# A long fp32 transformer kernel: the order of its steps planned by strands and kept durations in place of hand-set rates

## The reference

```python
# first_block: one layer
h = rmsnorm(x, norm1_g); proj = h @ w_in          # q, k, v (8 heads of 64), f_logit, u
attn = forgetting_attention(q, k, v, cumsum(log_sigmoid(f_logit + b_forget)))   # causal
pool = multiscale_pool(u, w_pool, pool_scale)     # trailing means over 2, 4, 8, 16 tokens
x = x + concat([attn, pool]) @ w_out
h2 = rmsnorm(x, norm2_g); x = x + (silu(h2 @ w_gate) * (h2 @ w_up)) @ w_down     # 2816 hidden
x = rmsnorm(x, final_g)
# second_block: layer 0 with diff_attention (8 heads, two maps each), layer 1 with mla_attention (16 heads, latents)
for i in (0, 1):
    x = x + (diff_attention, mla_attention)[i](rms_norm(x, attn_norm_g[i]))
    x = x + conv_ffn(rms_norm(x, ffn_norm_g[i]))  # up, causal convolution of 3 taps, silu(g) * val, down; 2816 hidden
return rms_norm(x, final_norm_g)
```

## Time and profile before

| what | value |
|---|---|
| median of 3 runs | 1991.57 us (1990.54 to 1992.43) |
| profiled execution, own time | 1996.32 us |
| its span, first to last instruction | 1994.2 us |
| mean granted TensorE clock | 0.971 of full speed |
| PE busy | 1884.0 us, 8953 matmuls |
| DVE, ACT, POOL busy | 1126.4, 793.9, 159.3 us |
| DMA | 152 MB, 76 GB/s over the span |

### The profile page before, as it was taken

How to read it: one execution, slowest core, us unless ns; L and a number is a source line. 1 busy time by engine, 2 the same in 40 slices (tenths; PEclk the granted TensorE clock), 3 DMA queues, 4 the chain that set the end, 5 groups by cost and what they waited for, 6 DMA issues and landing times.

```text
span 1994.2 us, 23116 instructions
## 1 busy us (share of the span) xinstructions
PE 1884.0 (94%) x8953; PEld 1551.3 (78%) x8953; DVE 1126.4 (56%) x1886; ACT 793.9 (40%) x1406; POOL 159.3 (8%) x155
## 2 busy tenths in 40 slices
PE   7997999999999899988999999998888799999998
PEld 6786778888887788877888888787777678888886
DVE  4557644344345666686663654646676676557365
ACT  4444432122234454443442432446545354234142
POOL 3002110000004100102000000023000020000001
PEclk9999999999999999988999999998898999999998
DMA  4211222332322112111322223221011022223322
GB/s 140 71 59 43 64 85 95 95 95 95 94 92 83 59 49 73 53 32 44 106 92 92 92 95 95 86 75 48 23 43 32 23 93 93 92 92 94 95 95 74
DMA packets 127769, 152.17 MB, mean 76 GB/s; under 512 B 9322, under 2 KB 98956, under 8 KB 127660
## 3 DMA queue, kind: packets, MB, share of 16 engines
q1 hardware_dynamic: 127384, 150.59, 23.9%
q10 hardware_dynamic: 276, 0.10, 0.0%
HBM read 148.50 MB, written 2.10 MB: 76 GB/s over the span
## 4 chain that ended last, share of the span: by engine, by line
PE 82%; DVE 8%; ACT 5%; issue 3%; POOL 2%; DMA 0%; SPq 0%; POOLq 0%; DVEq 0%; ACTq 0%
PE bk L1360 21%; PE bk L1361 21%; PE bk L1362 21%; PE bk L1388 4%; PE bk L1389 4%; PE bk L1390 4%; PE bk L1365 3%; DVE SM L1552 1%; ACT FS L1729 1%; DVE PT L1499 1%; POOL FS L1784 1%; ACT R L1668 1%; ACT WH L1664 1%; DVE R L1499 1%; DVE XT L1505 1%
## 5 line engine op out<-in xcount | busy, mean ns | idle before, releaser
L1360 PE MATMUL bk<-R,WH 128*128 128x512 f32 x1812 | 726.0, 401 | 16.4 <-DVE R L1499 10.9
L1361 PE MATMUL bk<-R,WH 128*128 128x512 f32 x1812 | 719.7, 397 | 0.0
L1362 PE MATMUL bk<-R,WL 128*128 128x512 f32 x1812 | 719.6, 397 | 0.0
L1494 DVE TENSOR_TENSOR WL<-RAW,WH 128x1024 fp32r<-128x1024 f32 (+3 forms) x282 | 352.7, 1252 | 634.5 <-ACT WH L1664 632.5
L1664 ACT ACTIVATE WH<-RAW 128x1024 fp32r<-128x1024 f32 (+3 forms) x282 | 293.8, 1042 | 641.4 <-PE bk L1362 589.1
L1360 PEld LDWEIGHTS bk<-R,WH 128*128 128x128 f32 x1812 | 342.7, 189 | 101.4 <-issue 20.2
L1362 PEld LDWEIGHTS bk<-R,WL 128*128 128x128 f32 x1812 | 342.2, 189 | 83.9
L1361 PEld LDWEIGHTS bk<-R,WH 128*128 128x128 f32 x1812 | 342.7, 189 | 80.3
L1388 PE MATMUL bk<-WH,R 128*128 128x512 f32 (+4 forms) x528 | 191.4, 362 | 7.8 <-DVE R L1486 4.3
L1784 POOL TENSOR_TENSOR FS<-FS 128x512 f32<-128x512 f32 x56 | 89.2, 1595 | 1341.4 <-ACT FS L1688 1338.3
L1389 PE MATMUL bk<-WH,R 128*128 128x512 f32 (+4 forms) x528 | 183.2, 347 | 0.0
(11 more groups left out here) (126 smaller groups left out, 1702.9 us busy)
## 6 DMA issues: line engine op xcount, KB each, us to landing
RAW<-in_ffn_w_up_dram SPq DMA_DIRECT2D x176, 256.0 KB, 3.0
RAW<-in_ffn_w_down_dram SPq DMA_DIRECT2D x44, 512.0 KB, 3.7
RAW<-in_w_gate_dram SPq DMA_DIRECT2D x44, 256.0 KB, 2.9
RAW<-in_w_up_dram SPq DMA_DIRECT2D x44, 256.0 KB, 3.1
RAW<-in_w_down_dram SPq DMA_DIRECT2D x22, 512.0 KB, 3.7
RAW<-in_da_w_qkv_dram SPq DMA_DIRECT2D x32, 256.0 KB, 3.0
RAW<-in_w_in_dram SPq DMA_DIRECT2D x17, 256.0 KB, 3.2
RAW<-in_w_out_dram SPq DMA_DIRECT2D x8, 512.0 KB, 3.6
```

Source lines behind the costliest of these rows:

```text
L1360: e.matmul(dst, lh, rh, start=start, stop=False)
L1361: e.matmul(dst, lh, rl, start=False, stop=False)
L1362: return e.matmul(dst, ll, rh, start=False, stop=stop)
L1494: e.tensor_tensor(WL[:, s, 0:m], RAW[:, r, 0:m], WH[:, s, 0:m].bitcast(F32), ALU.subtract).then_inc(on["wlo_dve"], 1)
```

## The change

The steps and what they compute stay. What appends them is replaced. Every line of work becomes a strand, a generator that yields its next step with all that the step waits for: one for each attention unit, for each map's max and exp, for each head's value product and output, for each evicted bank, for each turned head, for the high and the low weight halves, and one, `products`, that runs through all dense products from the first to the last. For every engine the plan keeps a time at which it is free (`free_at`), and for every semaphore value a time at which it is reached (`ready_at`), from durations kept for each kind of step (`takes`) and fixed delays (`LAG`, `HIDDEN`). `run` asks every strand for the beginning of its next step, takes the earliest, and among the steps of the same engine that could begin within `PATIENCE` of it the one of lowest rank: 0 for gates, norms and the reservation of tiles, 1 for attention, evictions and turns, 2 for weight halves and squares, 3 for `products`. Within a rank the strand that was made first wins. Steps that held several engines in turn (`root`, `gate_in`, `lam`) are cut into one step for each engine. Products may hold 5 of the 8 banks in attention stages (8 elsewhere) and other steps 4. An attention unit may begin when no more than `lag` units are between it and the last one turned. Tiles for queries, values and outputs are reserved in the order of the groups.

The diff, cut to its core; lines that only pass such strands on are left out:

```diff
...
-    "square": {"act": 1}, "acc": {"pool": 1}, "sums": {"pe": 1}, "root": {"dve": 5, "act": 2},
+    "square": {"act": 1}, "acc": {"pool": 1}, "sums": {"pe": 1}, "root_in": {"dve": 1}, "root_exp": {"act": 2}, "root_out": {"dve": 4},
...
+LAG = {"pe": 100.0, "act": 40.0, "dve": 40.0, "pool": 120.0}
+HIDDEN = {"pe": 0.0, "act": 85.0, "dve": 80.0, "pool": 0.0}
+PATIENCE = {"pe": 100.0, "act": 60.0, "dve": 60.0, "pool": 0.0}
...
+def takes(kind, eng, f):
+
+    def mm(n):
+        return max(110.0, n / 2.19)
+
+    def act(n, cols=0):
+        return 170.0 + 93.0 * cols + 0.83 * n
+
+    def dve(n):
+        return 150.0 + 1.04 * n
+    if eng == "pe":
+        if kind == "gemm_f":
+            return 3 * len(f["xs"]) * mm(512)
...
+        return {"wlo": 1273.0, "add": 682.0, "tap1": 743.0, "tap0": 743.0, "settle": 745.0, "diag": 880.0, "root_in": 165.0,
...
-        later, lates = [], []
-
-        def tick():
-            while lates:
-                lates.pop(0).both()
-
-        def pump(n=1):
-            tick()
-            for _ in range(n):
-                if later:
-                    later.pop(0)()
...
+        def begins(eng, after):
+            return max([free_at[eng]] + [at_time(d) + LAG[eng] for d in after])
+
+        def emit(kind, **fields):
+            t = None
+            for eng, n in SIGNALS[kind].items():
+                name = f"{kind}_{eng}"
+                fields[eng + "0"] = made.get(name, 0)
+                made[name] = fields[eng + "0"] + n
+                newest[eng] = fields[eng] = (on[name], made[name])
+                if n:
+                    t = max(t or 0.0, begins(eng, fields.get("after", ())))
+                    t += takes(kind, eng, fields)
+                    ready_at[id(on[name]), made[name]] = t
+                    free_at[eng] = t - HIDDEN[eng]
+            st = Step(kind, fields)
+            steps.append(st)
+            return st
...
+        def spawn(gen, rank=1):
+            serial[0] += 1
+            strands.append(Strand(gen, (rank, serial[0])))
...
+                can = []
+                for s in strands:
+                    if s.next is not None:
+                        eng = next(iter(SIGNALS[s.next[0]]))
+                        can.append((begins(eng, s.next[1].get("after", ())), eng, s))
+                if not can:
+                    assert not strands, [s.gen.__qualname__ for s in strands]
+                    break
+                t, eng, _ = min(can, key=lambda x: (x[0], x[2].rank))
+                s = min((x for x in can if x[1] == eng and x[0] <= t + PATIENCE[eng]), key=lambda x: x[2].rank)[2]
+                kind, fields = s.next
+                s.go(emit(kind, **fields))
+                if s.over:
+                    strands.remove(s)
+
+        tiles, fsl, banks = Ring(NT), Ring(NFS), Ring(NB)
+        taken = {"gemm": 0, "one": 0}
+        cap = {"gemm": NB, "one": 4, "kept": 0}
+
+        def bank(use="one"):
+            while not banks.fr or taken[use] >= cap[use]:
+                yield None
+            taken[use] += 1
+            b = banks.get()
+            b.use = use
+            return b
...
+            hi = yield step("hi", dst=dst_h, src=src, scale=1.0 if scale is None else scale, after=counts([*after, *free]))
+            lo = yield step("lo", dst=dst_l, src=src, high=dst_h, scale=scale, after=[hi.act])
+            return lo.dve
...
-        def split_chunk(n):
-
-            if n >= NRAW:
-                w_split[n - NRAW].both()
-            free = counts([w_used[n - NSP]] if n >= NSP else [])
...
+        def high_weights():
+            for n in range(len(chunks)):
+                while n >= NSP and n - NSP not in w_used or n >= NRAW and n not in lands:
+                    yield None
+                free = [w_used[n - NSP]] if n >= NSP else []
+                w_split[n] = yield step("whi", n=n, after=[(s_raw[n % NRAW], landed[n]), *free])
+
+        def low_weights():
+            for n in range(len(chunks)):
+                while n not in w_split:
+                    yield None
+                st = w_split[n]
+                lo = w_low[n] = yield step("wlo", n=n, after=[st.act])
                 if n + NRAW < len(chunks):
                     emit("load", n=n + NRAW, of=lo)
-                return lo
-            w_split[n] = Halves(hi, low)
-            lates.append(w_split[n])
+                    lands[n + NRAW] = True
+                    coming(n + NRAW, at_time(lo.dve))
...
-        def run(*gens):
-            gens = [[g, n, 0] for g, n in gens]
-            while gens:
-                for gw in sorted(gens, key=lambda x: (x[2] + 1) / x[1]):
-                    said = next(gw[0], "end")
-                    if said == "end":
-                        gens.remove(gw)
-                    if said != WAIT:
-                        gw[2] += 1
-                        break
-                else:
-                    wanted()
...
+                    if bk[m] is None:
+                        bk[m] = yield from bank("gemm")
+                    st = yield step("gemm_f", n=n, m=m, bank=bk[m].i, xs=[(x.h.i, x.l.i) for x in xs], start=k == 0,
+                                    stop=k + nk == nk_total, after=counts([split, *[x.ready for x in xs], *(bk[m].free if k == 0 else [])]))
                     if m == nm - 1:
                         w_used[n] = st.pe
-                    pump(rate)
-                    yield
+                    if k + nk == nk_total:
+                        spawn(evict(m0 + m, bk[m], st.pe))
...
+                while state.scored < u or u > state.turned + lag or not (G.turned and G.gated and flags.consts and h < G.heads):
+                    yield None
...
+                while state.headed < u // 4 - 1 or state.turned < u:
+                    yield None
+                b = yield from bank()
...
-        run((attention([A0, A1], "fg", 2), 72), (pool_part(), 24 + 16 + 8 + 4 + 16))
-        fsl.put(FG.ckf, newest["act"])
-        tiles.put(FG.cq, newest["pe"])
-        flush()
-        N = Norm(g=V_N2)
-        run((residual(A1.O, 2, N), 1))
...
+            cap["gemm"], cap["kept"] = 5, 3
+            yield from qkv_group(A0, 0, N, "fg", False)
+            spawn(gates(), 0)
+            attention([A0, A1], "fg", 2)
+            yield from qkv_group(A1, 1, N, "fg", False, A0)
+            yield from gemm_f(N.X, 8, 4, ev_pool(N))
+            N.free_x(newest_use())
+            N.shut = True
...
+            spawn(settle(ND))
+            spawn(lam_sums())
+            cap["gemm"] = 5
+            attention(Gs, "da", 3)
+            for g in range(4):
+                prior, before = (Gs[g - 1] if g else A1), (Gs[g - 2] if g > 1 else None)
+                yield from qkv_group(Gs[g], g, ND, "da", g == 3, prior, before, first_part() if g == 2 else None)
...
-        run((mla_group(Gs[0], 0), 1))
-        later.extend([kpe_down(n) for n in range(4, 8)])
-        run((attention(Gs, "mla", 4), 144), (seq_mla(), 70))
...
+            attention(Ms, "mla", 4)
+            for g in range(4):
+                yield from mla_group(Ms[g], g, Ms[g - 1] if g else None, Ms[g - 2] if g > 1 else None)
+            for g in (1, 2):
+                yield from till(Ms[g])
+                yield from residual(Ms[g].O, 2)
+            yield from till(Ms[3])
+            N4 = Norm(g=V_FN + 8)
+            yield from residual(Ms[3].O, 2, N4)
+            cap["gemm"] = NB
...
+        spawn(products(), 3)
+        run()
...
```

More of the change, by code:

```diff
@@ L88 @@
     heads = 8
-    tflog = None
 class Slot:
@@ new lines, in kpe @@
+            fsl.put(s, st.pool)
+            b = yield from bank()
+            st = yield step("heads", bank=b.i, c0=576, width=96, after=counts([b.free, st.pool, lat.toks]))
+            lat.ups.append(st.pe)
+            lo = yield from halves(KT[64:96, 0, :], KT[64:96, 1, :], BK[b.i][64:96, :], [st.pe], None, kfree[0] + kfree[1])
+            lat.k[0] = lo
+            put_bank(b, lo)
+            for n in range(1, 8):
+                st = yield step("kpe_copy", i=2 * n, after=counts([lo, kfree[2 * n], kfree[2 * n + 1]]))
+                lat.k[2 * n] = st.pool
```

1545 lines of the change are left out of this document (812 added, 733 removed).

## The result

| what | before | after |
|---|---|---|
| median of 4 runs each, same chip | 1991.11 us (1990.54 to 1992.43) | **1870.47 us** (1866.51 to 1872.75) |
| ratio, 95% interval | | **0.9391** (0.9373 to 0.9409) |
| profiled span | 1994.2 us | 1867.3 us |
| PE busy | 1884.0 us (94%) | 1828.3 us (98%) |
| PE idle (span less busy) | 110 us | 39 us |

The changed kernel is faster by 121 us. The span fell by 126.9 us: 71 of it is idle time of PE, 56 is busy time of the same 8953 matmuls. The cause of the other 9 is not shown.

A forecast was written before the change was run, and what follows sets the result against it. PE, busy 94%, was taken as the bound, with only its idle and half-clock time, mostly in attention, to win. Terms -25 - 12 - 8 - 7 = -52 took the profiled 1996.3 us to 1944, median 1940; range 1900 to 1990.

The forecast's parts named there:

- the value product's wait and the rotation's wait: PE's waits for low halves of probabilities (third attention, 5.7 us piece) and POOL's rotation (second's entry, 6.1 us) would go.
- the third attention's -25: Stretch 1373.4 to 1588.7 us: better order takes it from 215 to about 190, two thirds of a possible 38.
- the 9.3%: Loose share (idle plus half-clock time) mid second attention, the old trace's best mixing, used to price the third at 177 us.
- rival 1: Mixing goes further in the attention stages, about as tight as the trace's best stretches: -90, 1902 us; chance 0.16.
- The LDWEIGHTS rule: Third attention: headroom judged by LDWEIGHTS busy share, 73% against 80%, would allow 195 us, at most -20; not adopted.
- -12 and -8: Second attention: -12 at its end, residuals filling the last head's bare 8 us chain; -8 at its entry, POOL waits covered.
- First attention: -7: First attention, 77.7 to 253.7 us: a third of its 21.4 us loose time won, bounds +5 and -16.
- Feed-forward: 0: Feed-forward parts: nothing to win; prepared weight chunks cover the eviction burst and low half with 2.6 us to spare.
- Banks: 0: Attention stages: cap of 5 of 8 banks for products, 4 for others, costs 0, at most 20 us.
- Rival 2: Attention stages: buffers and DVE limit, attention then products run alone; only the entry is won, 1983 us; chance 0.20.
- Rival 3: Feed-forward blocks: weight splits starve on DVE behind evictions, 3.5 us a block, +25, 2017 us; chance 0.11.
- Rival 4: Whole kernel: plan knows one clock, chip grants two, queues drift and waits only change places, 1990 us; chance 0.06.

The follow-up runs named there:

- dense first: Changed kernel with dense products and weight halves raised to attention's rank 1, winning ties against it; 1996.1 us, ratio 1.0016.
- longer lag: Changed kernel with third-attention lag 5, 8 banks for other steps, no patience and earlier landing times for the first two weight chunks; 1858.5 us, ratio 0.9322.
- max twice: Changed kernel with each max of the third attention done a second time on DVE, unused, 64 more instructions; 1889.7 us, ratio 0.9478.
- walls: Changed kernel with products held after the first group of the second and third attention until its heads are turned; 1876.5 us, ratio 0.9415.
- rank only: Changed kernel with endless patience, so an engine's lowest rank goes next however late it can begin; 2248.9 us, ratio 1.1278.
- raised rates: Kernel before the change, old planner, with attention's rates raised fourfold (288, 288, 576); 2023.0 us, ratio 1.0142.

## Why the prediction was right or wrong

**What held.** The places: 59.2 + 42.9 + 14.5 of the 126.9 us come out of the attention stages. The signs that it named: the value product's wait and the rotation's wait are gone (0.3 us each), the third stage's clock is 1.00, and a dense stretch has its 216 matmuls in 50 us, as in the earlier trace rows:

```profile
300.00:350.00 50.00, 50.00 (x216) 40.18 (x215) 18.60 (x21) 11.94 (x13) 0.00 (x0) 1.00 0.32 98
```

The reason for the third attention's loss, "one of order": with the same buffers and rank alone undone (dense first), 41 of its 59 us are lost again. The sign that did not come true is the time of that attention, about 190 us: 25 was too little.

**The step that failed: the third attention's -25.** It measured -59.2 over the stage, at least 53.5 of it in the stretch that was priced. The mechanism was right and the size wrong, and the step that made it so is the 9.3%. The work at full clock was nearly right: the whole stage by the same reckoning is 258.03 - 0.08 x 294.9 = 234.4 us, and it takes 235.7. It is no floor, though: longer lag has the stage in 230.0. I did not believe that it could be reached, for two reasons, both wrong here. First I took 9.3% loose, the old trace's best mixing, as the limit; it was a product of the old order, and the new one leaves 3.9 of 235.7, 1.7%. Then I took a third off because DVE would be fuller, and held against rival 1 that "two engines near 80% do not interlock without gaps". Over 170 us of this stage they do, with 2.2 us of gaps, and in its best stretch nearly without any:

```profile
1400.00:1450.00 50.00, 49.96 (x313) 44.66 (x312) 47.88 (x118) 34.60 (x91) 2.64 (x4) 1.00 0.10 33
```

PE 49.96 and DVE 47.88 of the same 50 us. The limit was not far: with 24 us more of DVE (max twice) gaps of 12 us in 170 are back.

**The LDWEIGHTS rule.** The bound that I drew from the Trainium skill, "Perfetto Trace Analysis", "Identifying the Most-Contended Engine", at most -20 for this term, was still tighter, and the measurement decides against it. The section names the share of peak arithmetic beside the LDWEIGHTS share, which the prediction does not mention, and gives no share that counts as full: the 80% came from the trace. PEld is busy 204.57 of 235.7 us in the third stage, 87%, more than the 298.72 of 371.40, 80%, of a dense stage like the one that I had taken as full.

**Second attention: -12 and -8, together -20; measured -42.9.** The end was sized by the bare chain and halved, the entry about right by its rows, and the middle (11.4 us loose in 122.7) was put at nothing, as the standard for the rest. It was the same mistake: 180 us of this stage now run with 0.3 us idle. By the windows the loose time fell at the entry from 13.6 us to 2.3 (0.6 idle and 0.04 x 42.7), at the end from 24.0 to 4.9, and between them to 0.3. The reason that I gave for the entry was wrong too: walls puts the run-on at 2.5 us here and leaves the rotation covered. By the timelines it is covered because it begins earlier and runs beside the group's own products: 28.7 us after the first of them, before 40.5 (POOL of the changed kernel, then of the one before).

```profile
625.97 1.37 POOL L1941 TENSOR_TENSOR TOK<-TOK,CN 128x256 f32<-128x256 f32 x1 [15.46 <-ACT TOK L1851]
```
```profile
656.46 0.68 POOL L1788 TENSOR_TENSOR TOK<-TOK,CN 128x256 f32<-128x256 f32 x1 [21.38 <-ACT TOK L1702]
```

**First attention: -7; measured -14.5 with the start**, which lost 3.8 us up to the first dense product; the gain of all that follows is 18.3, past the bound of -16. I had left the first 30 us as they were, and priced neither the order of the first turns nor that the plan needs landing times for the first loads, which were kept too late. The largest wait that I named there, 5.5 us, is the sum of two, the longest of them 4.1.

**Feed-forward: 0; measured -10.2 together.** The cover of 2.6 us held: over the first of them PE is busy 371.40 of 371.40 us. Before, the first took 375.6 us with PE busy 373.23; I had called this "Nothing to win" for all three.

**Banks: 0.** No cost shows: PE is idle 0.3 us in 180 of the second attention, where the caps apply.

**Rivals.** Rival 1 (1902) named the right direction but had the same 9.3% in its price, and so fell short too. Rival 2 did not come. The Trainium skill ("Perfetto Trace Analysis", "Optimization Strategy") says that the same gap coming back can mean too little SBUF or PSUM for the next tile. Here that would have been the wrong lead: both kernels have the same 34 tiles, 9 slots of FS, 8 banks and 2 and 3 weight slots, and the gaps are gone. The two phases of this rival are real, though, as dense first shows, when the products go first. Rival 3 did not come either, and its place is real: with one duration for all steps PE waits 174 us in the feed-forwards for low weight halves. Rival 4 did not come: PE's clock is granted at 0.994, so that there was little for the queues to drift from. Wrong durations do cost time: at 30% two thirds of the gain are lost.

**What stays open.** How the gain splits between idle time and clock was only read from the traces, not tried apart; whether the caps on banks are needed; and whether DVE's time or each unit's chain limits the third stage next.

## What to carry to other kernels

Where two engines share a stage and neither is full, estimate the gain of a better order from the fuller engine's own work at full clock, not from the tightest stretch that the old order happened to reach. It is an estimate and no strict floor. A plan that takes the step which can begin first, with measured durations for each kind, and gives ties to the chain with the long latencies so that dense work fills the rest, came within 1% of that estimate in the third stage (235.7 against 234.4; longer lag went below it, 230.0); priority without beginning times (rank only, raised rates), beginning times with dense work first, and durations by engine alone each left the whole kernel no faster than before, though some stages kept a part. Such a plan is as good as its durations: measure them, those of the first loads too.

## What the runs showed of the hardware

With enough dense work between the steps of attention, PE, loading weights for 44.66 of 50 us, kept starting matmuls beside a DVE busy 47.88 of them; I had expected gaps there. And the lower clock did not stay where it had been: in the third stage the granted clock was 0.92 with PE idle 36.9 us, and is 1.00 with 3.9, on the same instructions. In dense first it is 1.00, 0.83 and 0.62 in stretches of 30 us in which PE is idle 0, 8.2 and 12.0 us. The idle time alone does not give it: two other stretches of that run have 1.00 with 4.2 us idle and 0.94 with 7.1. So closing the gaps was paid twice: 71 us as the gaps themselves, and at most about 47 as clock.
